# The expert stage of a two-block transformer kernel, rewritten in units of 512 columns

## The reference

```
logits = xt @ w_router                     # 256 x 8
top_w, top_idx = softmax of the two largest logits
order = argsort of the token-expert pairs by expert
h  = silu(xs @ w_gate[e]) * (xs @ w_up[e])  # 1024 -> 2816, for each expert e
ys = (h @ w_down[e]) * top_w                # 2816 -> 1024
out[token] = sum of its two ys
```

## Time and profile before

| | us |
|---|---|
| median of 3 runs | 2968.67 |
| the profiled execution | 2973.35 |
| its span | 2971.6 |
| TensorE busy | 2598.4 (87%) |
| VectorE busy | 1714.6 (58%) |
| ScalarE busy | 1274.9 (43%) |
| read from HBM | 605.83 MB, 204 GB/s over the span |

### The profile page before, as it was taken

How to read it: one execution, slowest core, us unless ns; L and a number is a source line. 1 busy time by engine, 2 the same in 40 slices (tenths; PEclk the granted TensorE clock), 3 DMA queues, 4 the chain that set the end, 5 groups by cost and what they waited for, 6 DMA issues and landing times.

```text
span 2971.6 us, 33909 instructions
## 1 busy us (share of the span) xinstructions
PE 2598.4 (87%) x11836; PEld 2023.3 (68%) x11836; DVE 1714.6 (58%) x2044; ACT 1274.9 (43%) x1714; POOL 68.2 (2%) x88
## 2 busy tenths in 40 slices
PE   4978997767998998998999798988996998898996
PEld 2646874446776776776776686887874786687884
DVE  2446454455886886886787645535554554455545
ACT  1233432324665665665666333343431442043441
POOL 1000000000000000000000000000001000000001
PEclk7989998887999999999999899989998999999998
DMA  7816548724996996997899453406543643325551
GB/s 294 310 59 222 172 158 308 254 71 137 324 327 234 318 328 228 329 327 268 297 327 311 151 202 133 136 36 212 173 159 98 207 170 108 133 69 186 188 180 53
DMA packets 397402, 608.89 MB, mean 205 GB/s; under 512 B 14112, under 2 KB 317248, under 8 KB 390592
## 3 DMA queue, kind: packets, MB, share of 16 engines
q1 hardware_dynamic: 389648, 583.32, 57.3%
q0 software_dynamic: 6288, 22.55, 2.2%
q10 hardware_dynamic: 1312, 1.05, 0.1%
HBM read 605.83 MB, written 1.05 MB: 204 GB/s over the span
## 4 chain that ended last, share of the span: by engine, by line
PE 60%; DVE 17%; issue 12%; ACT 5%; DMA 4%; POOL 1%; ACTq 0%; DVEq 0%; SPq 0%
PE G L663 34%; PE A L663 18%; DVE w_lo L1876 9%; PE TB L663 4%; ACT w_hi L1463 4%; PE TB L685 2%; DMA wide<-in_moe_w_up 1%; PE TB L1036 1%; DVE hidden L1927 1%; DMA wide<-in_w_in 1%; DMA wide<-in_ada_w 1%; PE TB L935 1%; DVE small L2094 1%; DMA small<-in_c 1%; DVE x_tok L2106 1%
## 5 line engine op out<-in xcount | busy, mean ns | idle before, releaser
L1876 DVE TENSOR_TENSOR w_lo<-wide,w_hi 128x1024 fp32r<-128x1024 f32 x572 | 675.0, 1221 | 69.6 <-ACT w_hi L1463 65.3
L663 PE MATMUL G<-w_hi,u_hi 128*128 128x512 f32 x1584 | 646.6, 408 | 15.7 <-DVE u_lo L1901 6.4
L663 PE MATMUL G<-w_hi,u_lo 128*128 128x512 f32 x1584 | 621.9, 393 | 0.0
L663 PE MATMUL G<-w_lo,u_hi 128*128 128x512 f32 x1584 | 621.8, 393 | 0.0
L1463 ACT ACTIVATE w_hi<-wide 128x1024 fp32r<-128x1024 f32 x572 | 578.1, 1052 | 38.6 <-PE G L663 12.4
L663 PEld LDWEIGHTS G<-w_hi,u_hi 128*128 128x128 f32 x1584 | 299.8, 189 | 106.1 <-DVE w_lo L1876 34.9
L663 PEld LDWEIGHTS G<-w_hi,u_lo 128*128 128x128 f32 x1584 | 299.4, 189 | 66.0
L1876 DVE TENSOR_TENSOR w_lo<-down,w_hi 128x1024 fp32r<-128x1024 f32 x286 | 337.2, 1220 | 11.1 <-ACT w_hi L1463 10.4
L663 PEld LDWEIGHTS G<-w_lo,u_hi 128*128 128x128 f32 x1584 | 300.3, 190 | 57.9 <-issue 1.9
L663 PE MATMUL A<-w_hi,hidden_hi 128*128 128x512 f32 x792 | 317.3, 401 | 10.7 <-DVE w_lo L1876 10.7
L663 PE MATMUL A<-w_hi,hidden_lo 128*128 128x512 f32 x792 | 315.2, 398 | 0.0
(11 more groups left out here) (252 smaller groups left out, 2919.1 us busy)
## 6 DMA issues: line engine op xcount, KB each, us to landing
wide<-in_moe_w_gate SPq DMA_DIRECT2D x88, 1024.0 KB, 5.5
wide<-in_moe_w_up SPq DMA_DIRECT2D x88, 1024.0 KB, 8.5
down<-in_moe_w_down SPq DMA_DIRECT2D x88, 1024.0 KB, 9.4
wide<-in_ffn_w_in SPq DMA_DIRECT2D x88, 1024.0 KB, 7.6
wide<-in_ada_w SPq DMA_DIRECT2D x48, 1024.0 KB, 7.1
down<-in_ffn_w_out SPq DMA_DIRECT2D x44, 1024.0 KB, 8.5
wide<-in_w_in SPq DMA_DIRECT2D x24, 1024.0 KB, 6.9
wide<-in_fox_w_in SPq DMA_DIRECT2D x12, 1024.0 KB, 5.2
```

The costliest lines, as they stand in the source:

```text
L663: return nc.tensor.matmul(o, lhsT, rhs, start=start, stop=stop, skip_group_check=True)
L1876: V.tensor_tensor(w_lo[to][:, :], raw, w_hi[to][:, :].bitcast(F32), ALU.subtract).then_inc(lo_ready, 1)
```

## The change

A unit now has 512 columns, with its gate products in bank 0 of `G` and its up products in bank 1; 2816 columns are five such units and one of 256, whose gate and up stand side by side as before ("both"). All pieces of a pair are numbered in one list (`PIECES`, 132 of them): the eight up pieces of a unit, then the four down pieces of the unit before. Rounded pieces go round a ring of six, each freed by TensorE's count `moe_used`. Raw pieces have rings of eight (up) and four (down), and SP loads each piece by itself, 512 KB, as soon as the piece that lay there has been split.

ScalarE and VectorE walk the same list. Before a piece they wait until TensorE has used the piece six places back, and do what belongs behind it (`behind`): silu, the split of the turned hidden values, the product. `turn` of a unit now stands between the gate and the up products of the next. The gather serves both experts of a pair at once, from `src` split in two halves in the router stage (`l_hi`, `l_lo`), in four quarters, and stands between the last two down products of the pair before. The scatter of each expert but the last stands between the gate and up products of later units. The loop over pairs is written out on TensorE, ScalarE and VectorE; SP keeps it.

Below are added lines, without blank ones; "..." marks what is left out. The removed lines are for the greatest part those of the functions printed above. `unit_chunks(u)` is 4, and 2 for the sixth unit. The unpacked path is rewritten in the same units and is not shown.

```diff
+UNITS = 6
+WCOLS = 512
+RING = 6
+WIDE_RING = 8
+DOWN_RING = 4
+def expert_pieces():
+    order = []
+    for e in range(2):
+        for u in range(UNITS):
+            order += [("both", e, u, q) for q in range(4)] if u == UNITS - 1 else \
+                [(kind, e, u, q) for kind in ("gate", "up") for q in range(4)]
+            behind = (e, u - 1) if u else ((0, UNITS - 1) if e else None)
+            if behind:
+                order += [("down", *behind, q) for q in range(unit_chunks(behind[1]))]
+    return order + [("down", 1, UNITS - 1, q) for q in range(unit_chunks(UNITS - 1))]
...
-        pack = sb("pack", 2048)
+        pack = sb("pack", 2560)
+        pack_at = nc.sbuf_base - 4 * 2560
+        pick_w = pack[:, 512:1024].rearrange("p (e t s) -> p e t s", e=2, t=T)
+        put_back = pack[:, 1024:1536].rearrange("p (e s) -> p e s", e=2)
+        packed_out = pack[:, 1536:2560]
...
+        def raw_piece(n, at):
+            kind = PIECES[at][0]
+            if kind == "down":
+                j = DOWN_PIECES.index(at)
+                return down[j // 2 % 2][:, (j % 2) * 1024:(j % 2 + 1) * 1024], moe_down_full[j % DOWN_RING], j, DOWN_RING
+            j = UP_PIECES.index(at)
+            return (wide[(n.w + j // 4) % RW][:, (j % 4) * 1024:(j % 4 + 1) * 1024], moe_full[j % WIDE_RING], j, WIDE_RING)
...
+                    sp.wait_ge(lo_ready, n.lo - 4)
+                    with sp.Fori(0, PAIRS) as i:
+                        for at, (what, e, u, q) in enumerate(PIECES):
+                            dst, full, j, ring = raw_piece(n, at)
+                            same = DOWN_PIECES if what == "down" else UP_PIECES
+                            before = same[j - ring] if j >= ring else same[j - ring] - PAIR
+                            sp.wait_ge(lo_ready, i * PAIR + (n.lo + before + 1))
+                            if j == 4 and what != "down":
+                                sp.wait_ge(lo_ready, n.lo)
...
+                            elif what == "both":
+                                halves = dst.rearrange("p (k h f) -> p k h f", k=2, h=2)
...
+                                for h, part in enumerate((w, up)):
+                                    sp.dma_start(halves[:, :, h], kview(part)[:, 2 * q:2 * q + 2, u * WCOLS:FF]) \
+                                        .then_inc(full, 16)
+                            else:
+                                sp.dma_start(dst.rearrange("p (k f) -> p k f", k=2),
+                                             kview(w)[:, 2 * q:2 * q + 2, u * WCOLS:(u + 1) * WCOLS]).then_inc(full, 16)
+                    for half in range(2):
+                        released[half - RW] = (lo_ready, n.lo + (PAIRS - 1) * PAIR + UP_PIECES[84 + 4 * half - 1] + 1)
...
+                def up_piece(p, kind, e, u, q, bank):
+                    at = PIECE_AT[kind, e, u, q]
+                    pe.wait_ge(lo_ready, n.lo + p * PAIR + at + 1)
+                    for kk in range(2):
+                        k = 2 * q + kk
+                        row = e * 1024 + k * P
+                        last = mm3(G[:, bank, :], uh[:, row:row + P], ul[:, row:row + P],
...
+                    last.then_inc(moe_used, 1)
+                def down_product(p, e, u):
+                    pe.wait_ge(moe_lo, p * 2 * UNITS + e * UNITS + u + 1)
+                    if u == 0 and p:
+                        pe.wait_ge(moe_added, 2 * (2 * p + e - 1))
+                    for q in range(unit_chunks(u)):
+                        at = PIECE_AT["down", e, u, q]
+                        pe.wait_ge(lo_ready, n.lo + p * PAIR + at + 1)
                         for half in range(2):
...
+                        last.then_inc(moe_used, 1)
+                def turn(p, e, u):
+                    unit = p * 2 * UNITS + e * UNITS + u
+                    pe.wait_ge(moe_product, unit + 1)
+                    if unit > 1:
+                        pe.wait_ge(moe_lo, unit - 1)
+                    if e == 0 and u == 3:
+                        pe.wait_ge(moe_back, p + 1)
+                    for f in range(unit_chunks(u)):
+                        last = nc.tensor.transpose(TB[:, unit % 2, tok(f)], gated[:, unit % 2, tok(f)], ident)
+                    last.then_inc(moe_turned, 1)
...
+                def scatter(p, e, t, bank):
+                    pe.wait_ge(moe_packed, 2 * p + e + 1)
+                    if t and bank == 2 * e:
+                        pe.wait_ge(moe_added, 2 * (2 * p + e) + 1)
                     for half in range(2):
...
+                    last.then_inc(moe_scattered, 1)
+                def gather(p):
+                    pe.wait_ge(moe_picked, p + 1)
+                    if p:
+                        pe.wait_ge(moe_added, 2 * (2 * p - 1))
+                    for j in range(4):
+                        for half, evacuated, at in ((l_hi, moe_u_hi, 0), (l_lo, moe_u_lo, 1)):
+                            if p or j:
+                                pe.wait_ge(evacuated, 4 * p + j)
+                            for cc in range(2):
+                                for t in range(T):
+                                    last = mm(A[:, at, cc * S:(cc + 1) * S], half[t][:, tok(2 * j + cc)],
+                                              pick[:, t * S:(t + 1) * S], t == 0, t == 1)
+                            last.then_inc(moe_gathered, 1)
+                def gates(p, e, u):
+                    unit = p * 2 * UNITS + e * UNITS + u
+                    if e == 0 and u == 0:
+                        pe.wait_ge(moe_u_hi, 4 * (p + 1))
+                        pe.wait_ge(moe_u_lo, 4 * (p + 1))
+                    if unit:
+                        pe.wait_ge(moe_silu, unit)
+                    for q in range(4):
+                        up_piece(p, "gate", e, u, q, 0)
+                def ups(p, e, u):
+                    unit = p * 2 * UNITS + e * UNITS + u
+                    if unit:
+                        pe.wait_ge(moe_product, unit)
+                    for q in range(4):
+                        up_piece(p, "up", e, u, q, 1)
+                pe.wait_ge(acc_free, n.free)
+                pe.wait_ge(moe_src_hi, T)
+                pe.wait_ge(moe_src_lo, T)
+                gather(0)
+                for p in range(PAIRS):
+                    for e in range(2):
+                        for u in range(UNITS - 1):
+                            gates(p, e, u)
+                            before = unit_before(e, u)
+                            if before:
+                                turn(p, *before)
+                            if u in (1, 2) and (p or e):
+                                scatter(*((p, 0) if e else (p - 1, 1)), u - 1, 0 if e else 2)
+                            if e == 0 and u == 3:
+                                turn_weights(p)
+                            ups(p, e, u)
+                            if before:
+                                down_product(p, *before)
+                        unit = p * 2 * UNITS + e * UNITS + UNITS - 1
+                        pe.wait_ge(moe_product, unit)
+                        up_piece(p, "both", e, UNITS - 1, 0, 1)
+                        up_piece(p, "both", e, UNITS - 1, 1, 1)
+                        turn(p, e, UNITS - 2)
+                        up_piece(p, "both", e, UNITS - 1, 2, 1)
+                        up_piece(p, "both", e, UNITS - 1, 3, 1)
+                        down_product(p, e, UNITS - 2)
+                    turn(p, 1, UNITS - 1)
+                    if p < PAIRS - 1:
+                        gather(p + 1)
+                    down_product(p, 1, UNITS - 1)
+                scatter(PAIRS - 1, 1, 0, 2)
+                scatter(PAIRS - 1, 1, 1, 0)
...
+                def round_piece(p, at):
...
+                    nc.scalar.activation(w_hi[at % RING][:, :], raw, ACT.Copy).then_inc(hi_ready, 1)
+                def silu(p, e, u, bank, cols):
+                    unit = p * 2 * UNITS + e * UNITS + u
+                    if unit:
+                        act.wait_ge(moe_product, unit)
+                    nc.scalar.activation(sg[:, 0:cols], G[:, bank, 0:cols], ACT.Silu).then_inc(moe_silu, 1)
+                def turned(p, e, u):
+                    unit = p * 2 * UNITS + e * UNITS + u
+                    cols = unit_chunks(u) * P
+                    act.wait_ge(moe_turned, unit + 1)
+                    nc.scalar.activation(hth[:, 0:cols], TB[:, unit % 2, 0:cols], ACT.Copy).then_inc(moe_hi, 1)
...
+                def outputs(p, e):
+                    if p or e:
+                        act.wait_ge(moe_scattered, 2 * (2 * p + e))
                     nc.scalar.activation(packed_out, A[:, 2 * e:2 * e + 2, :].rearrange("p h c -> p (h c)"), ACT.Copy) \
+                        .then_inc(moe_packed, 1)
+                def gathered(p, j):
+                    act.wait_ge(moe_gathered, 8 * p + 2 * j + 1)
+                    nc.scalar.activation(uh[:, :].rearrange("p (e k s) -> p k e s", e=2, k=KD)[:, 2 * j:2 * j + 2],
```

(100 more changed lines are left out.)

532 lines of the change are left out of this document (234 added, 298 removed).

## The result

| | before | after |
|---|---|---|
| median, us | 2968.94 (4 runs, 2967.88 to 2971.71) | 2868.37 (4 runs, 2861.87 to 2872.81) |
| the profiled execution | 2973.35 | 2867.43 |
| its span | 2971.6 | 2865.6 |

The ratio of the times is 0.9658 (0.9642 to 0.9673): 101 us less, where 112 were forecast (2857.0; range 2838 to 2898). The time lies in the range and the sign is right; one term of the sum, the gather, was too small, and two smaller ones were too large.

The account below looks back on a forecast made before the run. TensorE was taken to lose time inside and between expert pairs. Units 747.2, weights 2.4, scatter 26.0, gathers 18.0, clock 5.4 and waits 6.0 made 805.0 us, ending the stage 111.9 us earlier: 2857 us, range 2838 to 2898.

Parts of the forecast that it names:

- the gather: Between a pair's last two down products, four quarters waiting on copies: 6.0 us each, bounds 3.9 and 9, three making 18 us.
- The unit: Expert stage: 72 products and 4 transposes take 16.98 us, as in the dense stages; four pairs 747.2 us.
- Unnamed waits: Expert stage: 1.5 us a pair, 6.0 in all, for waits without a named cause; between 0 and 16.9.
- Scatter: Between gate and up products: 3.71 us per expert, seven inside the stretch, 26.0 us.
- the loss of clock: Idle time at the gather may slow the twelve products behind it: 1.8 us three times, 5.4 us, bounds 0 and 5.4.
- the signs that I named: Expected in the profile: turns 17 us apart, gathers about 6 us, DMA share below 0.95, nearly no ScalarE wait for loads.
- Start: First gate product of the expert stage: 1.7 us earlier, at 711.5 instead of 713.25; bounds 709 and 715.
- Written-out loop: At pair ends, writing out the engines' loops over pairs removes 5.93 us of issue and the wait for one-hots.
- Transfers: Expert stage loads need 343 GB/s; 397 taken for 2 KB rows, bounds 330 and 397, so no bound.
- the transfer rival: Expert stage: the queue holds only 330 GB/s over long stretches, so 91 us gained, 2877; chance 0.14.
- the VectorE case: Expert stage remainders: mild waiting gives about 2924, chance 0.12; a pause at every piece 3077, chance 0.05 together with late loads.
- the change doesn't do what it says: At pair ends, gather or written-out code costs what the loop did: 4 x 10 us more, 2897; chance 0.03.

## Why the prediction was right, and where not

*The unit.* 16.98 us from the dense stage; measured 17.00. This is about half of the gain: 88 units of 9.13 us and 44 of 17.00 differ by 55.4 us, of the 106.9 by which the stage's end moved. The handovers of silu, product and split cost nothing in it, as costed. The turn experiment shows the larger part of the cause directly: with the old unit size and nothing but the turn and its splits moved, the 9.13 us become 8.73 and 30.2 us go.

*Unnamed waits.* I added 6.0 us. There are none inside the pairs, and only the last down product of the stage waits, 1.1 us for hidden_lo. *Scatter.* 1.72 per half, 3.44 per expert instead of 3.71.

*The gather is the term that was mis-sized.* Three gathers with the loss of clock were 18.0 + 5.4 = 23.4 us and measure 12.0 + 11.2 + 10.9 = 34.0, and the three down products behind them take 1.1 us more than their 2.81 each: 35.1, or 11.7 more than forecast. The working held that each load is issued when the piece 8 to 20 places earlier has been split; for the last down loads that is 4 places, and SP's queue, which I called free, had them and its own loop turn ahead of the next pair's gate loads. SP's loop stands in no term of the sum. With that loop written out the gathers are 6.9, 6.8 and 6.5 us, at the full clock. The loss of clock was foreseen but mostly in the wrong place: the quarters of the gather itself run at half, and the down product behind it at full speed (a product every 0.23 us), but for its first three products at the first pair's end (0.43 us each). Of the signs that I named, two did not hold at the pairs' ends: the gather of about 6 us, and nearly no wait of ScalarE for a load (14.6 us in 9 times for gate loads).

*The sum.* 805.0 us forecast from first gate to last down product, 809.6 measured: 11.7 more for the gathers with their clock, 6.0 less for waits, 1.9 less for scatter, and 0.8 left over, among it the last wait (1.1 more), the units (44 times 0.02 more) and the transposed weights (0.44 us each instead of 0.60). That the sum is off by only 4.6 us is luck in part: the waits that I couldn't name cancel half of what the gather lacked. *Start* 711.9 against 711.5. The profiled execution came out 6.0 us above the forecast for it. The rest of the median's 11.4 is the offset: I took the 4.7 us between the profiled execution of before and its median over, and the profiled execution of after lies 0.9 below its own median.

*Written-out loop.* By the 5.93 us of issue at each of three ends it should give 17.8; alone, in the kernel before, it gives 15.6.

*Transfers.* No bound, as forecast (341 GB/s, share 0.93), but for a wrong reason. I took the row length to make the difference between 348 and 397 GB/s. Two rows refute it: 1 KB runs carry 359 GB/s for 160 us and, in the kernel before with its turn moved, 360 for 40 us. The 330 GB/s of the earlier trace rows at a share of 0.98, on which the transfer rival stood, were what the kernel asked for, not what the queue could give. The Trainium skill (DMA: Bandwidth & Descriptors, section "Measured") asks for transfers of 1 MiB and more, from measurements of DMAs that GpSimd issues. SP issues those of this case. Here loads of 512 KB and 256 KB give the same time, and windows with loads of 1 MB, 512 KB and 256 KB all carry 359 to 363 GB/s; the measurement decides. A 512 KB load lands 6.4 to 8.0 us after its issue in the kernel after, and one is issued about every 1.5 us (140 in 204.7 us), so by this estimate four or five are in flight.

*The rivals.* VectorE is busy 706.4 of 802.1 us, 0.88, as worked out, and TensorE never waits for w_lo in the stage of the kernel after: neither form of the VectorE case came. That the change doesn't do what it says is out as well.

*What the gain is made of.* Made alone in the kernel before, the turn gives 30.2 us and the loop 15.6. If they add, 55 of the 101 are left, and how these divide was not run; what follows is an estimate from the traces. From the end of the last but one down product to the next pair's first gate product the turn experiment takes 27.4 + 27.1 + 27.2 = 81.7 us and the kernel after 14.8 + 14.9 + 13.8 = 43.5. Of these 38 us the loop is 15.6; about 23 are the last down product, scatter, adding and gather that stood in line there. A further 20 are the units, 88 times 8.73 - 8.50. The 12 left are not divided; late up loads at the pairs' starts, for which ScalarE waits 10.8 us in the turn experiment, are one candidate.

## What to carry to other kernels

When engines take turns within a unit, put the turn among the next unit's products before anything else: of the edits made alone it gave the most, 30.2 us, and it needs no new tile sizes. When a loop is written out on the compute engines, look at the queue that feeds them too, and count what stands in it ahead of the next loads. Written out there it gave 10.2 us as long as the work behind it had no cover, and nothing that the runs can tell apart once the gather was spread. Work that goes back and forth between engines step by step (a gather in quarters) belongs between steps of other work; in the same place at one piece it took 7 to 12 us, spread over the down product it took little more than its own 4 (2.1 us of waits in all three ends).

## What the runs showed of the hardware

- SP's loop turn shows as 3.27 to 3.83 us of issue, beside the 5.93 of the compute engines. With it gone the whole kernel is 10.2 us faster, over three pair ends.
- After 4.69 us without work the granted clock was 0.52 from 1112.0 to 1117.5, so nearly all of it at 1.2 GHz, and each group of four products of 256 columns took 0.98 to 1.02 us instead of 0.56 (start to start); after waits of up to 0.76 us it stayed at 1.00:

```profile
1112.00:1117.50 5.50, 5.22 (x21) 4.48 (x22) 3.73 (x6) 2.25 (x4) 0.00 (x0) 0.52 1.05 391
```

```profile
900.00:907.00 7.00, 5.08 (x36) 4.26 (x35) 5.30 (x7) 4.24 (x7) 0.00 (x0) 1.00 1.05 387
```

The first is a window of the kernel after, the second of the one with SP's loop written out.
- A DMA share of 1.0 is no proof of a full queue: 0.98 went with 330 GB/s in the kernel before, and 1.05 with 360 for the same loads once the turn was moved; in the kernel after 0.99 went with 363 and 1.05 with 391.
